# Input projection of a two-block network on one core: queries and keys by input tile, eight output tiles at a time

## The reference, cut to what matters

```python
hn = rms_norm(h, mixer_norm_g[layer])          # x * rsqrt(mean(x*x) + eps) * g
proj = h @ w_in                                # 1024 -> 2560
q, k, v, g, u = jnp.split(proj, [512, 1024, 1536, 2048], axis=-1)
q = rope(q, positions)
k = rope(k, positions) * (Dh ** -0.5)
scores = einsum(q, k) * decay_mask             # four heads, two chunks of 128
```

## Time and profile before

| | |
|---|---|
| median of 3 runs | 1123.86 us (1123.34 to 1124.85) |
| profiled execution, its own time | 1123.79 us |
| its span, first to last instruction | 1122.0 us |
| TensorE busy | 1114.8 us, 99% |
| VectorE busy | 834.9 us, 74% |
| ScalarE busy | 609.5 us, 54% |
| GpSimd busy | 44.9 us, 4% |
| moved by DMA | 203.53 MB, mean 181 GB/s |

### The profile page before, as it was taken

One profiled execution on the slowest core, in us unless ns is written; L12 is line 12 of the kernel. 1 busy time (PEld: TensorE's weight loads), 2 busy tenths in 40 slices (PEclk: granted clock), 3 DMA queues, 4 the chain that ended last, 5 costly groups with the idle time before them and its releaser, 6 DMA issues.

```text
span 1122.0 us, 18843 instructions
## 1 busy us (share of the span) xinstructions
PE 1114.8 (99%) x7338; PEld 993.4 (89%) x7338; DVE 834.9 (74%) x1287; ACT 609.5 (54%) x951; POOL 44.9 (4%) x67
## 2 busy tenths in 40 slices
PE   9999999999999999999999999999999999999998
PEld 9999888888876988888899998888888789888887
DVE  7977877766775878777658867877665887877753
ACT  5645566554542756555544455666544677655631
POOL 4030000000000000000000000000001210000000
PEclk9999999999999999999999999999999999999999
DMA  8545555555494455556544645555654425555552
GB/s 308 190 156 186 176 193 191 191 195 184 154 282 112 151 182 194 188 188 211 180 172 159 217 151 188 191 189 188 222 183 155 140 86 188 185 191 188 183 198 70
DMA packets 35368, 203.53 MB, mean 181 GB/s; under 512 B 4176, under 2 KB 10576, under 8 KB 11984
## 3 DMA queue, kind: packets, MB, share of 16 engines
q1 hardware_dynamic: 35136, 202.32, 52.1%
q10 hardware_dynamic: 144, 0.01, 0.0%
HBM read 200.09 MB, written 2.23 MB: 180 GB/s over the span
## 4 chain that ended last, share of the span: by engine, by line
PE 94%; DVE 3%; DMA 1%; ACT 1%; issue 0%; SPq 0%; DVEq 0%; ACTq 0%
PE banks L419 46%; PE banks L428 24%; PE banks L397 5%; PE banks L403 5%; PE banks L400 5%; PE banks L460 4%; PE banks L443 1%; PE banks L449 1%; PE banks L446 1%; DMA raw_t<-w 1%; DVE lo_t L328 1%; PE banks L1595 0%; DVE lo_t L315 0%; DVE scr L1354 0%; PE banks L1581 0%
## 5 line engine op out<-in xcount | busy, mean ns | idle before, releaser
L328 DVE TENSOR_TENSOR lo_t<-raw_t,hi_t 128x1024 fp32r<-128x1024 f32 x364 | 439.4, 1219 | 28.5 <-ACT hi_t L322 27.4
L322 ACT ACTIVATE hi_t<-raw_t 128x1024 fp32r<-128x1024 f32 x364 | 374.9, 1050 | 125.6 <-PE banks L428 82.0
L419 PE MATMUL banks<-x,hi_t 128*128 128x512 f32 x1536 | 370.6, 392 | 0.0
L419 PEld LDWEIGHTS banks<-x,hi_t 128*128 128x128 f32 x1536 | 281.8, 188 | 55.3 <-issue 0.8
L428 PEld LDWEIGHTS banks<-x,lo_t 128*128 128x128 f32 x1536 | 198.5, 191 | 8.5
L428 PE MATMUL banks<-x,lo_t 128*128 128x256 f32 x1536 | 201.1, 283 | 0.0
L419 PE MATMUL banks<-f,hi_t 128*128 128x512 f32 x704 | 166.4, 390 | 0.0
L419 PEld LDWEIGHTS banks<-f,hi_t 128*128 128x128 f32 x704 | 129.9, 188 | 25.5
L545 DVE TENSOR_TENSOR scr<-banks,scr 128x512 f32<-128x512 f32 x88 | 60.8, 691 | 82.9 <-ACT scr L613 82.1
L428 PEld LDWEIGHTS banks<-f,lo_t 128*128 128x128 f32 x704 | 89.2, 191 | 2.8
L428 PE MATMUL banks<-f,lo_t 128*128 128x256 f32 x704 | 90.1, 283 | 0.0
(11 more groups left out here) (197 smaller groups left out, 1073.2 us busy)
## 6 DMA issues: line engine op xcount, KB each, us to landing
raw_t<-w SPq DMA_DIRECT2D x182, 1024.0 KB, 4.9
scr<-shifts SPq DMA_DIRECT2D x32, 142.0 KB, 4.1
raw_t<-w SPq DMA_DIRECT2D x3, 512.0 KB, 10.0
shifts<-scr SPq DMA_DIRECT2D x8, 144.0 KB, 3.5
h<-xT SPq DMA_DIRECT2D x4, 256.0 KB, 7.7
out<-h SPq DMA_DIRECT2D x8, 128.0 KB, 4.3
cst<-consts SPq DMA_DIRECT2D x1, 816.0 KB, 12.8
raw_t<-w SPq DMA_DIRECT2D x2, 256.0 KB, 5.3
```

What stands on the lines that cost most here:

```text
L322: e.activation(hi_t[:, p % RING, :], raw_of(p), ACT.Copy).then_inc(s_hi, 1)
L328: e.tensor_tensor(lo_t[:, p % RING, :], raw_of(p), hi_t[:, p % RING, :].bitcast(F32), ALU.subtract).then_inc(s_lo, 1)
L419: m = e.matmul(halves(banks[:, to[j], :]), hi_t[:, slot, r * P:(r + 1) * P], parts[:, ks[j], :, :], start=ks[j] == 0, stop=False, skip_gro ...
```

## The change

- 17 filler products in place of 21.
- `pe_first_tiles(k)` now does all eight output tiles (banks 0 to 3) for input tile k, in two halves of four, so queries and keys take one piece for each input tile; the second loop over banks 2 and 3 is gone. The weights of this part are stored in that order.
- Pieces 0 to 3 are still split in halves, pieces 4 on whole.
- Loads: piece 1 ahead of x tiles 2-3, pieces 2 and 3 ahead of x tiles 4-5, and x tiles 6-7 behind chunk 2.
- The column sums stand ahead of input tile 6, the spread ahead of the second half of input tile 7: 16 and 4 output-tile steps before the end of the part, as before.
- VectorE's order after xl of input tile 5: four angle operations, lo 5, xl 6, `gg`, lo 6, xl 7, the four steps of line 746, lo 7, the four closing operations, then as before lo 8, the mean and the scaled identities.
- All four banks of queries and keys are complete only after the last input tile: ScalarE's copies for every bank wait for tile 63, and its splits go up to another tile before each.

```diff
-WARM_START = 21
+WARM_START = 17
...
-            for n in range(1, EARLY):
-                e.dma_start(h[:, 2 * n:2 * n + 2, :], xT[:, 2 * n:2 * n + 2, :]).then_inc(s_x[n], 16)
-                part = slice(n % 2 * PIECE, n % 2 * PIECE + PIECE)
-                e.dma_start(raw_t[:, n // 2, part], w[n // 2, :, part]).then_inc(s_first[n + 1], 16)
+            for what in ("w1", "x1", "w2", "w3", "x2"):
+                n = int(what[1])
+                if what[0] == "x":
+                    e.dma_start(h[:, 2 * n:2 * n + 2, :], xT[:, 2 * n:2 * n + 2, :]).then_inc(s_x[n], 16)
+                else:
+                    part = slice(n % 2 * PIECE, n % 2 * PIECE + PIECE)
+                    e.dma_start(raw_t[:, n // 2, part], w[n // 2, :, part]).then_inc(s_first[n + 1], 16)
             load_chunk(e, 2)
+            e.dma_start(h[:, 6:8, :], xT[:, 6:8, :]).then_inc(s_x[3], 16)
...
                 act_xh(e, 0, k)
-                early_hi(e, k)
-            for p in range(EARLY, RING):
-                split_hi(e, p)
+                if k < EARLY:
+                    early_hi(e, 2 * k)
+                    early_hi(e, 2 * k + 1)
+                elif k < RING:
+                    split_hi(e, k)
...
-            for k in range(KD):
+            for k in range(EARLY):
                 dve_xl(e, 0, k)
-                early_lo(e, k)
+                early_lo(e, 2 * k)
+                early_lo(e, 2 * k + 1)
+            dve_xl(e, 0, 4)
             split_lo(e, EARLY)
+            dve_xl(e, 0, 5)
...
+            lo_to(e, 19)
+            dve_xl(e, 0, 6)
             e.wait_ge(s_col, 16)
             e.tensor_tensor(gg[:, :], ...
-            lo_to(e, 19)
+            lo_to(e, 27)
+            dve_xl(e, 0, 7)
             for c in (P1, P2, P3, P4):
                 e.wait_ge(dv.sem, n)
                 n = dv.mark(e.scalar_tensor_tensor(w1, kk, -c, w1, ALU.mult, ALU.add))
+            lo_to(e, 35)
...
+            for half in range(2):
+                js = range(4 * half, 4 * half + 4)
+                dsts = [banks[:, j // 2, (j % 2) * T:(j % 2 + 1) * T] for j in js]
+                if k == KD - 1 and half:
+                    pe_spread(e, 0)
+                early = k < EARLY and half == 0
+                e.wait_ge(s_hi_half if early else s_hi, k + 1)
...
+                e.wait_ge(s_lo_half if early else s_lo, k + 1)
...
             for k in range(KD):
+                if k == 6:
+                    pe_col_sums(e, 0)
                 pe_first_tiles(e, k)
-            for u in range(2, 4):
-                for t in range(2):
-                    for k in range(KD):
-                        c = 16 * u + 8 * t + k
-                        if c == 48:
-                            pe_col_sums(e, 0)
-                        if c == 60:
-                            pe_spread(e, 0)
-                        tile(e, G_QK + c, banks[:, u, t * T:(t + 1) * T], k, x2, k == 0, k == KD - 1)
...
-            for u, c in zip(range(4), (51, 59, 67, 75)):
+            for u, c in zip(range(4), (64, 67, 71, 75)):
                 hi_to(e, c)
-                e.wait_ge(s_tiles, upto(16 * max(u, 1) + 15))
+                e.wait_ge(s_tiles, upto(63))
...
-    parts = [wide(tiles(w_in[:, 0:1024]), 4), ...
+    parts = [wide(tiles(w_in[:, 0:1024]), 8), ...
```

More of the change, by code:

```diff
@@ L712, in act_start @@
             e.activation(st[:, 5, 0:1], one[:, 0:1], ACT.Copy)
+            e.wait_ge(s_col0, 16)
             for k in range(KD):
-                if k == 0:
-                    e.wait_ge(s_col0, 16)
                 if k % 2 == 0:
@@ L799, in pe_first_tiles @@
         def pe_first_tiles(e, k):
[L801 to L818, removed]
+            for half in range(2):
+                js = range(4 * half, 4 * half + 4)
+                dsts = [banks[:, j // 2, (j % 2) * T:(j % 2 + 1) * T] for j in js]
+                cols_of = [slice(j * P, (j + 1) * P) for j in js]
+                if k == KD - 1 and half:
+                    pe_spread(e, 0)
+                early = k < EARLY and half == 0
+                e.wait_ge(s_hi_half if early else s_hi, k + 1)
+                e.wait_ge(s_xh, x_done(0, k))
+                for j, dst, c in zip(js, dsts, cols_of):
+                    e.matmul(dst, hi_t[:, k % RING, c], x2[:, k, 0, :], start=k == 0 and j % 2 == 0, stop=False, skip_group_check=True)
+                e.wait_ge(s_xl, x_done(0, k))
+                for dst, c in zip(dsts, cols_of):
+                    e.matmul(dst, hi_t[:, k % RING, c], x2[:, k, 1, :], start=False, stop=False, skip_group_check=True)
+                e.wait_ge(s_lo_half if early else s_lo, k + 1)
+                for dst, c in zip(dsts, cols_of):
+                    m = e.matmul(dst, lo_t[:, k % RING, c], x2[:, k, 0, :], start=False, stop=k == KD - 1, skip_group_check=True)
@@ L820, in pe_retention @@
+            m.then_inc(s_tiles, 1)
         def pe_retention(e):
             for k in range(KD):
+                if k == 6:
+                    pe_col_sums(e, 0)
                 pe_first_tiles(e, k)
-            for u in range(2, 4):
-                for t in range(2):
-                    for k in range(KD):
-                        c = 16 * u + 8 * t + k
-                        if c == 48:
-                            pe_col_sums(e, 0)
-                        if c == 60:
-                            pe_spread(e, 0)
-                        tile(e, G_QK + c, banks[:, u, t * T:(t + 1) * T], k, x2, k == 0, k == KD - 1)
@@ L1958, in ffn @@
         return [wide(mixed(tiles(gate), tiles(up)), 2 * WIDE), flat(tiles(down))]
-    parts = [wide(tiles(w_in[:, 0:1024]), 4), flat(strips(w_in[:, 1024:1536])), flat(tiles(w_in[:, 2048:2560])),
+    parts = [wide(tiles(w_in[:, 0:1024]), 8), flat(strips(w_in[:, 1024:1536])), flat(tiles(w_in[:, 2048:2560])),
              flat(tiles(w_in[:, 1536:2048])), outer(a["mix_w_out"][0], (4, 5, 6, 7, 0, 1, 2, 3), N_RET)]
```

## The result

The changed kernel takes 1126.86 us (median of 10 runs, 1125.61 to 1127.99) against 1123.86 us (1123.29 to 1124.85): ratio 1.0025, 95% interval 1.0016 to 1.0033. The median is 3.0 us slower, over the 2.25 us that I had set as the border of "the same"; the interval runs from 1.8 to 3.7 us, so that it is slower is shown, and that it is past the border is not. The forecast time was 1125.6; the range, to 1128.0, holds the result. The profiled execution took 1125.61, its span 1123.8.

What follows compares the result with a forecast made beforehand. TensorE, busy 99% of the span, was taken as the bound, with VectorE the hidden second bound of this part. Strips 1.37 us later plus a 0.4 us stall gave +1.8 on 1123.79: 1125.6 us, range 1123.2 to 1128.0.

Steps and rivals of the forecast that it cites:

- the sum: VectorE's steps from lo 6 at 25.4 us take 8.54, identities ready at 33.94; strips of v start 1.37 us later.
- What starts lo 6: On VectorE, lo 6 waits for ScalarE's piece 6, which waits for chunk 3, kept at 24.15: ready at 25.4 us.
- rival C: Slower: chunk 3 lands at 25.3, or VectorE slows beside GpSimd, or its 1.0 us lag costs stalls: 1127.2 us, chance 0.12.
- The front: At TensorE's start, less filler lets real work begin at 7.4 us, 0.9 earlier, worth nothing if something later holds TensorE.
- The rope behind the mark: After the strips of v start, VectorE's first rope comes 2.1 us behind them; before, it was 1.13.
- VectorE's lag: From the first rope on, VectorE runs 1.0 us later against TensorE than before, 0.7 after idle time at 57.05.
- the stall of 0.4 us for lo 19: Near 69 us, TensorE waits for VectorE's lo of piece 19: 0.4 us, bounds 0 and 0.9.
- rival B: Slower: TensorE's idle stretch of 3.3 us ahead of the spread costs it its full clock: 1128.1 us, chance 0.10.
- My price of 2.5 us: Work lost by TensorE in the strips if they run at half pace for 5.1 us, as the filler did.
- A: No bubble: chunk 3 comes early or VectorE finds lo 6 ready; shift -0.4, no later stall: 1123.4 us, chance 0.24.
- D: Faster: identities ready in time, so 0.9 of filler and 2.2 of waits are won: 1120.7 us, chance 0.04.

Runs made afterwards that it cites:

- e2: The changed kernel with the four steps of range reduction (line 746) moved ahead of lo 6 on VectorE: 1124.14 us, ratio 1.0000.
- e3: The changed kernel with the mean right behind lo 7 and the scaled identities ahead of lo 8: 1124.60 us, ratio 1.0004.
- e5: The changed kernel with ScalarE waiting for `gg` behind its pieces 6 to 8 instead of ahead of piece 6: 1125.18 us, ratio 1.0009.
- e8: The changed kernel with GpSimd's squares cut to 8 of 256 columns, read for times alone: 1126.60 us.
- e7: The kernel before with 17 filler products, nothing else changed: 1123.65 us, ratio 0.9997.
- e10: The changed kernel with 21 filler products, as before the change: 1127.56 us, ratio 1.0030.
- e4: The changed kernel with 12 filler products in TensorE's idle stretch ahead of the spread: 1125.29 us, ratio 1.0011.
- e1: The changed kernel run again, unchanged: 1126.40 us, ratio 1.0020.
- e9: The changed kernel with the moves of e2 and e3, and ScalarE waiting for `gg` only behind the sines: 1122.46 us, ratio 0.9987.
- e6: The changed kernel with the moves of e3 and e5 together: 1124.47 us, ratio 1.0003.

## Why the prediction was right, and where it was not

**The bound and the sum: right, partly by luck.** The step that carried the forecast was that VectorE's order decides when the identities are ready: 33.94 forecast, 33.79 measured; strips at 35.80 forecast, 35.81 measured. e2 and e3 moved these instructions alone and moved the strips by 1.0 and 1.9 us (1.33 and 2.12 counted from `gg`). The steps from lo 6 to the identities were 8.54 us in the sum and are 33.79 - 25.54 = 8.25. The two terms that were too large are xl 7, 0.57 in the sum and 0.39 measured (the 0.57 had a short pause in it), and the four steps, 1.83 and 1.72.

**What starts lo 6: the wrong cause, the right number.** I had the landing of chunk 3, kept at 24.15. Issued 1.5 us earlier (11.3 against 12.8) it landed 0.65 us earlier, at 23.5, and ScalarE was held by `gg`, that is by VectorE, which then waited for ScalarE. The changed order of waits on ScalarE stood in the code: the wait for `gg` ahead of piece 6. It was there before, too, and there the chunk came later than `gg` (22.89 against 24.15), so rows 5 named the transfer. I had not asked what would be late next if the transfer came earlier. e5 settles it. `gg` itself came at 24.13 and not at 23.5: GpSimd's squares of x tiles 6-7 had moved beside lo 4 and the angle operations, and slowed them. The sum has no term for that; only rival C names it. e8 shows that it was wrong to leave it out, since that slowed work is what leads to `gg`. Against the sum the chunk came earlier and `gg` 0.6 us later, and lo 6 started at 25.54 where I had 25.4: that this number fits is luck.

**The front: right.** Real work at 7.56 (7.4 forecast), worth nothing at the end: e7 and e10. The loads were better than I took them to be (chunk 2 landed at 15.2, issued at 5.4, where before it landed at 18.0), and no input tile waited but one, for lo 5, 0.7 us.

**The rope behind the mark: overpriced.** I had the first rope 2.1 us behind the strips; it is 37.30 - 35.81 = 1.5. The term that failed is ScalarE's table load: I put it behind the angles, and it ran at 27.35, ahead of that wait. So VectorE's lag was 0.4 and not 1.0, it was gone by 58.44, and the stall of 0.4 us for lo 19 did not come: lo 19 ends at 68.14 and is first used at 68.46, the same slack as in rows 7. That the profiled execution nevertheless took the 1125.6 us forecast is chance: in place of the missing 0.4 us stand 0.77 us of clock near 364 less the 0.37 that the new order gains at 366, and the sum had neither.

**The clock: rival B was no rival but a part of the result.** I gave it 0.10 against the forecast, as an either-or. The runs show two losses in one: 1.6 us by the order (e4 against before, both at full clock; the rows give 1.0) and 1.1 us by the clock (e4 against e1). Together they make 2.7, and 2.4 and 3.0 were measured. The Trainium skill, "TensorE: Matmul & The Clock Gate", section "HAM oscillation — how this bites in real kernels", warns that behind a long enough gap the matmuls start at half clock; by that rule, e1's rows behind the gap agree, while the first profile shows that a gap of 3.04 us can also be passed at full clock. My price of 2.5 us was too high: 1.4 behind the gap in e1. And the chance was far too low: 21 of 21 executions had at least one such loss somewhere. With a fair chance for it, "slower" would have had more than its 0.38 and "same" less than its 0.58.

**Rivals A, C and D.** A is out: chunk 3 came 0.65 us early, not before 22.5, and `gg` held the piece. Of C's three conditions one was met, VectorE slowed beside GpSimd; the chunk was not late, and the strips and u had no stalls. Its time, 1127.2, is nearer to the median than the forecast's, but the rows do not bear it out, since the strips stand at 35.81 as forecast. D is out, though its tile order does give an early mark once VectorE's order allows it (e9): 2.2 us at the strips and 1.5 at the end, not 3.1.

**Why executions at 0.998 differ so much in time.** The kept profiles answer it in part. Near 364 each of them was at half clock for the same 3.4 us, and lost 0.71 to 1.33 us by it. Counted in the work done, the half clock began earliest in e6 and e2 (361.5 and 361.6), which lost most, and latest in e4 (362.4), which lost least, and the others stand in order between them. So the place of the half clock within that stretch sets its price.

What is open: how the gap and the fall 330 us behind it hang together, and why the kernels with the new order lack the gap of 0.47 us near 366. Also not tried: the old order of loads under the new order of tiles, so what share the loads have in chunk 2's 2.8 us is not told apart.

## What to carry to other kernels

When the unit with the slack is moved, ask of every in-order engine which instruction now stands behind a wait: four short operations queued behind a wait cost 1.3 us at the strips and, with the clock, 2.3 us of the median here, and moving them back cost nothing. An earlier mark is worth only what the engine that is the bound behind it can follow: e3 and e6 won it and gave it back, e9 kept 1.5 of 2.2 us. And a gap in TensorE's work has two prices, its length and the clock behind it; the mean granted clock of each execution shows the second where one profile may not.

## What the hardware showed that I had not expected

- Of 21 executions with a wait of 3 us on TensorE none kept the full clock; with waits of up to 0.9 us (e3, e4, e7, e9) 12 of 44 lost it, and 22 of 82 of the kernel before. In eight of the twelve kept profiles the clock fell near 364 us, in a stretch of small products; in seven of these TensorE waited there for no more than 0.3 us.
- In these kernels ScalarE's table load ran ahead of the wait for the angles where that wait stood alone (27.35 in the changed kernel, 26.58 in e8, 27.45 in e9), and behind it where three waits stood there (30.07 in e5, 30.63 in e6).
- Beside GpSimd's operations on SBUF an xl of VectorE takes 0.96 us instead of 0.48, a piece of lo 1.63 instead of 1.23.
